# Stick-breaking attention: neighbour differences taken once of the values, and no longer of each query's running product

## The reference

```python
z = einsum('bqhd,bshd->bhqs', q_blk, k) * scale
causal = key_pos[None, :] < t[:, None]
log_1m = where(causal, log_sigmoid(-z), 0.0)
excl = cumsum(log_1m, axis=3, reverse=True) - log_1m
a = where(causal, exp(log_sigmoid(z) + excl), 0.0)
o = einsum('bhqs,bshd->bqhd', a, v)
```

## Time and profile before

| | us |
|---|---|
| median of 3 runs (2195.93 to 2198.94) | 2198.15 |
| the profiled execution's own time | 2200.19 |
| its span in the trace | 2198.1 |
| TensorE busy in the span | 2061.5 (94%) |
| VectorE, ScalarE, GpSimd busy | 1087.3, 755.9, 233.9 |
| attention stage, first scores to first matmul of `sb_o` | 154.09 to 235.65 |

### The profile page before, as it was taken

One profiled execution on the slowest core, in us unless ns is written; L12 is line 12 of the kernel. 1 busy time (PEld: TensorE's weight loads), 2 busy tenths in 40 slices (PEclk: granted clock), 3 DMA queues, 4 the chain that ended last, 5 costly groups with the idle time before them and its releaser, 6 DMA issues.

```text
span 2198.1 us, 27172 instructions
## 1 busy us (share of the span) xinstructions
PE 2061.5 (94%) x10802; PEld 1664.2 (76%) x10802; DVE 1087.3 (49%) x1588; ACT 755.9 (34%) x1136; POOL 233.9 (11%) x290
## 2 busy tenths in 40 slices
PE   7988999999999988889999999998789889999997
PEld 6886788888888755558888888787579658888885
DVE  5336553433455755554534435766665445343444
ACT  4115442322332335553322324314552234232231
POOL 0008300000004123330000000001600000000000
PEclk9998999999999989899999999999899999999998
DMA  5220122222224410002222222221024112222221
GB/s 183 96 77 1 58 96 96 96 95 96 96 96 134 155 37 1 2 1 77 96 96 96 95 96 96 82 96 49 1 96 172 58 38 96 96 96 96 95 96 58
DMA packets 29701, 181.10 MB, mean 82 GB/s; under 512 B 4704, under 2 KB 5984, under 8 KB 8992
## 3 DMA queue, kind: packets, MB, share of 16 engines
q1 hardware_dynamic: 27216, 173.53, 22.6%
q0 software_dynamic: 1952, 6.03, 1.0%
q10 hardware_dynamic: 432, 0.11, 0.0%
HBM read 172.85 MB, written 2.10 MB: 80 GB/s over the span
## 4 chain that ended last, share of the span: by engine, by line
PE 82%; DVE 8%; ACT 4%; issue 3%; POOL 2%; DMA 0%; DVEq 0%; ACTq 0%; POOLq 0%
PE ps L408 24%; PE ps L410 24%; PE ps L409 24%; PE ps L1236 2%; PE ps L1216 2%; PE ps L1200 2%; POOL stick L746 1%; DVE w_lo L394 1%; PE ps L1398 1%; DVE left L713 1%; ACT n_probs L1269 1%; PE ps L803 1%; POOL f_probs L1157 1%; DVE f_probs L1058 1%; ACT w_hi L389 1%
## 5 line engine op out<-in xcount | busy, mean ns | idle before, releaser
L389 ACT ACTIVATE w_hi<-w_raw 128x2048 fp32r<-128x2048 f32 x160 | 305.4, 1909 | 606.7 <-PE ps L410 593.3
L408 PE MATMUL ps<-h_hi,w_hi 128*128 128x512 f32 x1200 | 472.4, 394 | 16.4 <-DVE h_lo L285 12.1
L409 PE MATMUL ps<-h_lo,w_hi 128*128 128x512 f32 x1200 | 468.6, 390 | 0.0
L410 PE MATMUL ps<-h_hi,w_lo 128*128 128x512 f32 x1200 | 468.3, 390 | 0.0
L394 DVE TENSOR_TENSOR w_lo<-w_raw,w_hi 128x2048 fp32r<-128x2048 f32 x160 | 367.1, 2294 | 173.0 <-ACT w_hi L389 172.6
L408 PE MATMUL ps<-o_hi,w_hi 128*128 128x512 f32 x1024 | 401.0, 392 | 5.3 <-DVE o_lo L888 2.5
L410 PE MATMUL ps<-o_hi,w_lo 128*128 128x512 f32 x1024 | 399.1, 390 | 0.0
L409 PE MATMUL ps<-o_lo,w_hi 128*128 128x512 f32 x1024 | 399.0, 390 | 0.0
L408 PEld LDWEIGHTS ps<-h_hi,w_hi 128*128 128x128 f32 x1200 | 226.1, 188 | 66.0 <-issue 17.5
L409 PEld LDWEIGHTS ps<-h_lo,w_hi 128*128 128x128 f32 x1200 | 226.2, 189 | 48.2 <-issue 1.7
L410 PEld LDWEIGHTS ps<-h_hi,w_lo 128*128 128x128 f32 x1200 | 226.2, 189 | 47.4
(11 more groups left out here) (270 smaller groups left out, 2301.4 us busy)
## 6 DMA issues: line engine op xcount, KB each, us to landing
w_raw<-in_wstream SPq DMA_DIRECT2D x160, 1024.0 KB, 4.8
x_res<-in_xT SPq DMA_DIRECT2D x4, 512.0 KB, 8.0
out_T<-x_res SPq DMA_DIRECT2D x8, 256.0 KB, 2.1
e_cmp<-kv_nat POOLq DMA_DIRECT2D x8, 128.0 KB, 7.0
k_slc<-kv_nat POOLq DMA_DIRECT2D x8, 128.0 KB, 2.6
k_win<-kv_nat POOLq DMA_DIRECT2D x8, 128.0 KB, 6.9
mem_in<-in_memT POOLq DMA_DIRECT2D x1, 1024.0 KB, 5.1
e_cmp<-kv_nat POOLq DMA_DIRECT2D x8, 127.8 KB, 7.2
```

The source lines that it names most:

```text
L389: act.activation(w_hi[:, par, :, :], w_raw[:, par, :, :], ACT.Copy).then_inc(hi_ready, 1)
L408: pe.matmul(o, l_hi, r_hi, start=first, stop=False)
L409: pe.matmul(o, l_hi, r_lo, start=False, stop=False)
L410: return pe.matmul(o, l_lo, r_hi, start=False, stop=last)
```

## The change

GpSimd no longer subtracts in each step. `stick` and `stickT` go; `left` has four slots instead of two, and TensorE transposes `left` itself as soon as the scan is done. `copy` writes `leftT` and takes 1 from each element on the way (bias -1.0). `beta(k)` waits for `turn(k-4)`, which frees its slot. Instead, GpSimd changes `sb_v` in place, a block of 256 columns (two pairs of heads) at a time, once VectorE has evicted it: two DMAs from GpSimd's queue copy the rows of `sb_v`, moved by one token, into `v_next` (127 partitions with four pieces of 1 KB each, and one partition with three pieces), and one subtraction of 128 x 1024 writes v[j-1] - v[j]. `values(k)` of the first step that uses a block waits for that subtraction (`k_v`). `v_next` has one buffer, so the four blocks follow one another.

```diff
-        left = place("left", [P, 2, 2, 5 * P], at=HOFF)
-        stick = place("stick", [P, 2, 2, 5 * P], at=HOFF + 10 * KB)
-        stickT = place("stickT", [P, 2, 2, 5 * P], at=HOFF + 20 * KB)
+        left = place("left", [P, 4, 2, 5 * P], at=HOFF)
+        leftT = place("leftT", [P, 2, 2, 5 * P], at=HOFF + 20 * KB)
+        v_next = place("v_next", [P, QT, BLK], at=NOFF)
...
             def turn(k):
-                pe.wait_ge(k_a, 2 * k + 2)
+                pe.wait_ge(k_scan, k + 1)
                 wait(pe, k_c, k)
...
-                                          stick[:, k % 2, e, at:at + P], ident[:, :])
+                                          left[:, k % 4, e, at:at + P], ident[:, :])
...
             def values(k):
...
                 if k % 2 == 0:
                     wait(pe, k_lo, p)
+                    pe.wait_ge(k_v, p // 2 + 1)
...
             def beta(k):
-                wait(act, k_a, 2 * (k - 1))
+                wait(act, k_t, k - 3)
...
-                act.activation(stickT[:, k % 2, :, :].rearrange("p a b -> p (a b)"), flat[:, 4 * S:4 * S + 10 * P],
-                               ACT.Copy).then_inc(k_c, 1)
+                act.activation(leftT[:, k % 2, :, :].rearrange("p a b -> p (a b)"), flat[:, 4 * S:4 * S + 10 * P],
+                               ACT.Copy, bias=-1.0).then_inc(k_c, 1)
...
-            for k in range(STEPS):
-                pool.wait_ge(k_scan, k + 1)
-                wait(pool, k_t, k - 1)
-                for i in (0, 1):
-                    t, at, w = segment(k, i)
-                    pool.tensor_tensor(stick[:, k % 2, :, at:at + w - 1], left[:, k % 2, :, at + 1:at + w],
-                                       left[:, k % 2, :, at:at + w - 1], ALU.subtract).then_inc(k_a, 1)
+            for i in range(4):
+                pool.wait_ge(tile_free, 4 + 2 * (b["sb_qkv"] + 9 + i))
+                here = sb_v[:, :, BLK * i:BLK * i + BLK]
+                if i == 0:
+                    pool.memset(v_next[0:1, 0, :], 0.0).then_inc(k_zero, 1)
+                pool.dma_start(v_next[1:P, :, :], here[0:P - 1, :, :]).then_inc(k_moved, 16)
+                pool.dma_start(v_next[0:1, 1:QT, :], here[P - 1:P, 0:QT - 1, :]).then_inc(k_moved, 16)
+                pool.wait_ge(k_zero, 1)
+                pool.wait_ge(k_moved, 32 * (i + 1))
+                pool.tensor_tensor(here, v_next[:, :, :], here, ALU.subtract).then_inc(k_v, 1)
+                pool.wait_ge(k_v, i + 1)
```

More of the change, by code:

```diff
@@ L193, in build_program @@
         hid_y, hid_hi, hid_ready = sem("hid_y"), sem("hid_hi"), sem("hid_ready")
-        k_mask, k_s, k_left, k_scan, k_a, k_t, k_c, k_pv, k_hi, k_lo = (sem("k_" + n) for n in (
-            "mask", "s", "left", "scan", "a", "t", "c", "pv", "hi", "lo"))
+        k_mask, k_s, k_left, k_scan, k_zero, k_moved, k_v, k_t, k_c, k_pv, k_hi, k_lo = (sem("k_" + n) for n in (
+            "mask", "s", "left", "scan", "zero", "moved", "v", "t", "c", "pv", "hi", "lo"))
         (st_qk, st_v, s_done, mx_ready, nm_ready, p_ready, den_ready, rc_ready, fac_ready, pn_ready, t_done,
@@ L660, in values @@
                         mm = pe.matmul(ps[HD * e:HD * e + HD, 7, P * t:P * t + P], sb_v[:, j, P * p + HD * e:P * p + HD * e + HD],
-                                       stickT[:, k % 2, e, P * n:P * n + P], start=(k % 2 == 0 and n == 0),
+                                       leftT[:, k % 2, e, P * n:P * n + P], start=(k % 2 == 0 and n == 0),
                                        stop=(k % 2 == 1 and n == 4))
@@ L685, in beta @@
                     act.wait_ge(k_s, 2 * k + i + 1)
-                    act.activation(left[:, k % 2, :, at:at + w], ps[:, 2 * i:2 * i + 2, 0:w], ACT.Sigmoid,
+                    act.activation(left[:, k % 4, :, at:at + w], ps[:, 2 * i:2 * i + 2, 0:w], ACT.Sigmoid,
                                    scale=-HD ** -0.5).then_inc(k_left, 1)
@@ L708, in vector_sb @@
         def vector_sb(dve):
-            backwards = lambda buf, k: buf[:, k % 2, :, :].rearrange("p a b -> p (a b)")[:, ::-1]
+            backwards = lambda buf, slot: buf[:, slot, :, :].rearrange("p a b -> p (a b)")[:, ::-1]
             def scan(k):
                 dve.wait_ge(k_left, 2 * k + 2)
-                dve.tensor_tensor_scan(backwards(left, k), backwards(left, k), backwards(stick_mask, k), 1.0,
+                dve.tensor_tensor_scan(backwards(left, k % 4), backwards(left, k % 4), backwards(stick_mask, k % 2), 1.0,
                                        ALU.mult, ALU.max).then_inc(k_scan, 1)
@@ L735, in pool_sb @@
                         pool.tensor_copy(stick_mask[:, a, e, at + w - P:at + w], m_stick[:, :]).then_inc(k_mask, 1)
-            pool.wait_ge(tile_free, 4 + 2 * b["sb_o"])
-            for a in (0, 1):
-                for i in (0, 1):
-                    t, at, w = segment(a, i)
-                    ins = pool.memset(stick[:, a, :, at + w - 1:at + w], 0.0)
-            for k in range(STEPS):
-                pool.wait_ge(k_scan, k + 1)
-                wait(pool, k_t, k - 1)
-                for i in (0, 1):
-                    t, at, w = segment(k, i)
-                    pool.tensor_tensor(stick[:, k % 2, :, at:at + w - 1], left[:, k % 2, :, at + 1:at + w],
-                                       left[:, k % 2, :, at:at + w - 1], ALU.subtract).then_inc(k_a, 1)
+            for i in range(4):
[9 more added lines that the diff above has]
+                pool.wait_ge(k_v, i + 1)
         def cross_units(q, k, v):
```

## The result

The changed kernel is slower. Its median is 2241.28 us (4 runs, 2235.40 to 2247.38) beside 2197.04 for the kernel before (4 runs): a ratio of 1.0201, 95% interval 1.0168 to 1.0234, so it is slower beyond the noise, by about 2%. The forecast was 2185.2, its range ended at 2203. The profiled execution took 2244.96 us, span 2242.8, clock 0.963.

The account below looks back on a forecast made before the run. Attention was taken as bound by scans and GpSimd subtractions running one after the other. Scan(4) at 169.86, five pairs of 8.61 and 9.75 put `sb_o` at 222.66, 13.0 us earlier: 2185.2 us, range 2179 to 2203.

Parts of the forecast that it names:

- The values' differences: GpSimd's block moves and subtractions: moves land in 2.4 to 7.7 us, a subtraction takes 1.89, first three blocks hidden.
- the sum: Attention stage's terms added up: first matmul of `sb_o` at 222.66 against 235.65, a gain of 13.0 us.
- the cover: The rest of the projection, behind which the first three blocks' moves were to be hidden, blocks evicted 11.5 us apart.
- the one engine: Rival for the 127-partition move: one DMA engine, 28.2 to 35.4 us a block, 2201 to 2230 us; chance 0.17.
- The sum without the moves: Attention stage's forecast apart from the price of the moves: pipeline filling, five pairs at 8.61 us, and a 9.75 us end.
- the ring: Attention loop's dependency cycle scan, low, values, turn, copy, beta, scan: 8.61 us a pair, taken as the new pace.
- the blocked scan: Early in attention, the last block's subtraction holds up a scan: 1.89 us counted, bounds 0 and 1.89.
- the filling: Start of attention: scans 0 to 3 back to back from 156.65, scan(4) at 167.97 with its beta already there.
- The copy's bias: Bias operand in ScalarE's copy: no change from 1.24 us expected; twice the time as upper bound.
- The clock: Rival: TensorE's clock falls after idling in attention, 1.6 us a fall, 2196.6 if in all seven pairs; chance 0.06.
- 1.00 from 154 on: Sign to look for: TensorE granted full clock in attention from 154 us on, against 0.92 before.
- TensorE's pace of 7.76: Rival: TensorE's own work sets the attention loop's pace, 7.76 us a pair, giving 2181 or 2179; chance 0.10.

Follow-up runs that it names:

- e1: Changed kernel with each block's big move cut into one of 126 partitions and one of a single partition: 2185.55 us.
- e3: Changed kernel without the moves and the subtraction of the values, so the loop is seen alone: 2180.65 us.
- e8: Changed kernel with the big move cut into four, one per tile of tokens, each 127 partitions with one 1 KB piece: 2185.60 us.
- e5: Changed kernel with the big move cut into 122 and 5 partitions: 2191.16 us.
- e6: e8 with low(m-3) ahead of scan(m) on VectorE: 2175.97 us.
- e11: The kernel before the change with only low(m-3) put ahead of scan(m) on VectorE: 2202.76 us.
- e4: Changed kernel with a move of 128 partitions, not shifted by a token and without edge rows: 2185.30 us.
- e7: Changed kernel with a separate buffer for each of the four blocks and subtractions after all the moves: 2199.56 us.

## Why the prediction was wrong

**The step that failed** is the price of the moves, in "The values' differences": "I take 2.4 to 7.7 us", from the moves of `e_cmp`. Those have one piece a partition and 64 partitions. The form here, 127 partitions with four pieces, lands in 32.4 to 39.9 us, and its issue alone takes GpSimd 4.6 us, for which the sum had nothing. From the step it followed that the blocks would be hidden by the projection of v; the cover would have been there, since e1, with one row cut off, lands in 4.8 us and gives 2185.55.

**The rival that came true** is the one engine (chance 0.17, 2201 to 2230). Its mechanism held: share 0.06, blocks in a row through one buffer, long waits at steps 8 and 12, but as long a one at step 4 too. Its size was short, 238.4 to 267.2 for `sb_o` against 279.90, for two reasons. The last block was ready at 269.91 and not by 261.0: the sum had no term for the first block's 45.1 us (119.76 to 164.84), whose move took 7.5 us longer to land, with the weights of the projection moving beside it, and which ended in a subtraction of 4.89 us between scans; the other three took 35.25, 34.98 and 34.84, inside the 28.2 to 35.4, with an issue of 4.6 us in them that I had not counted either. And values(12) to `sb_o` took 9.84 us and not 6.19, because TensorE was at 1.2 GHz after its wait. 8.9 + 3.65 is the 12.7 us above the upper end, but for 0.2.

**The chances.** The share for one engine was too low for what spoke for it: no row of before had more than one piece a partition, so the only rows that I held against it were of another form.

**The sum without the moves** was right. In e3 the ring is 8.56 (8.61 forecast) and `sb_o` comes at 221.27; the forecast without the blocked scan was 222.66 - 1.89 = 220.8. The blocked scan is 2.5 us in e8 (1.89 forecast). The subtraction itself takes 2.33 to 2.41 us and not 1.89. One premise of the filling was off by a little: scan(4) waits 0.99 us for its beta in e3, which the forecast had ready before. e1 and e8 end at 2185.55 and 2185.60 against 2185.2; part of that closeness is luck, since their stages are 12.0 us shorter than before and 13.0 were forecast.

**The other rivals.** The copy's bias costs nothing (1.24). The clock does not fall in the loop of e3 (1.00 from 176 to 221), whose waits are 0.84 us; it fell after the three long waits for `sb_v` in the changed kernel, and after 2.30 us idle in e8. The sign "1.00 from 154 on" was not met even so: among the first scores, from 156 to 160, e3 has 0.66 and 0.50, and the changed kernel 0.60 and 0.54. The length of one idle does not settle it: in e5 the rows after 2.34 us idle (213.67) are at full speed, and after 1.98 (193.43) the turn behind the values takes 2.35 us. Seven falls of 1.6 us are 11.2 us, where the prediction has 11.4. TensorE's pace of 7.76 is what e6 reaches, not the changed kernel.

**Where 58.7 us went** (125.75 - 67.04, against e3): 54.0 in waits for blocks; for the low clock 2.1 and 1.6 after the first two long waits (199.73 to 204.33 is 4.60 us and 234.92 to 239.00 is 4.08, not 2.49) and 3.65 after the third; less 3 x 0.84, the waits for `low` that are contained in the long ones. That sums to 58.8.

## What to carry to other kernels

Taking differences once of the values is worth 12 to 13 us here, and 19.7 of the stage with `low` ahead of the scan, if the move is cut so that it is spread over the DMA engines. A move between partitions has its price by its form, not by its bytes: look for the partition count and the pieces of each partition, and where no row of the trace has that form, hold the price open. When one bound goes, look for a second order of the same instructions: e11's edit lost 2.3 us before and gained 7.7 after.

## What the hardware showed that was not expected

- 127 partitions with four pieces of 1 KB each run on one DMA engine (DMA share 0.06), 122 on two (0.13), and 126 land in under 5 us with the row that was cut off; but 127 with one piece each land in 2.0 to 2.7 us.
- GpSimd's own time for the issue goes with it: 4.6 us for the one engine, 2.5 for two, 0.9 for 126 partitions and 0.8 for 128. So does the number of packets for the same bytes. From 110 to 290 us GpSimd's queue has 8320 packets in the changed kernel, 4224 in e5, 896 in e1 and 576 in e4, and the trace's packet records show what the difference is: 7620, 3460, 72 and none of them are of 16 bytes. In the changed kernel's second block they run until about 179 us (DMA share 0.24 from 170 to 176 us, at 14 GB/s) before the 4 KB packets run at their full rate.
- GpSimd's queue held its third such move until the first had landed (17.46 us), and everything behind it on GpSimd.
- Two moves of the one-engine form that overlap run beside each other: in e7 the third and fourth, issued 8 us apart, landed 5 us apart, in 36.4 and 33.5 us, at twice the share of one alone (0.13 and 0.06).
- A subtraction of 128x1024 takes 2.33 to 2.41 us alone and up to 4.89 beside the scans; a scan takes 2.83 alone and up to 4.92 when it comes second (e8, 159.22). "SBUF — State Buffer" of the Trainium skill, "Who interferes with whom", has a VectorE instruction with two inputs in SBUF, as the scan is, contend with a GpSimd instruction that reads SBUF, on a shared pair of ports; the rows agree.
